# A decoder layer with routed experts: rows gathered expert by expert, down projection split along its contraction, mixing on 32-row groups

## The reference, cut to what matters

```
p = rms_norm(x) @ w_in                       # 2048 -> 6144 columns
x = x + [attention | gated short conv] @ w_out
h = rms_norm(x)
g_star = argmax(h @ w_rg + b_rg)             # 1 of 4 groups
w, e_idx = top 2 of 8 experts in the group   # softmax weights
y = sum over the two experts of
      w * (silu(h @ w_gate[e]) * (h @ w_up[e])) @ w_down[e]
x = x + y
```

## Time and profile before

| | us |
|---|---|
| median of 3 runs (1517.11 to 1518.77) | 1518.23 |
| the profiled execution | 1517.3 |
| its span | 1515.5 |
| PE busy (88% of the span) | 1340.8 |
| DVE busy (26%) | 388.9 |
| ACT busy (14%) | 212.9 |
| POOL busy (4%) | 60.4 |

### The profile page before, as it was taken

How to read it: one execution, slowest core, us unless ns; L and a number is a source line. 1 busy time by engine, 2 the same in 40 slices (tenths; PEclk the granted TensorE clock), 3 DMA queues, 4 the chain that set the end, 5 groups by cost and what they waited for, 6 DMA issues and landing times.

```text
span 1515.5 us, 19525 instructions
## 1 busy us (share of the span) xinstructions
PE 1340.8 (88%) x8104; PEld 907.2 (60%) x8104; DVE 388.9 (26%) x842; ACT 212.9 (14%) x555; POOL 60.4 (4%) x65
## 2 busy tenths in 40 slices
PE   6999999999899968888978979869869879878887
PEld 6888888888677756446437437436426526535542
DVE  3333137765111141121122113103103113113112
ACT  4111231321001121100110110100100110110110
POOL 0000003312010000000000000000000000000000
PEclk9999999999999979889899879889889979979988
DMA  9965334637694326999999999999999999999997
GB/s 296 355 209 181 133 126 157 235 112 261 216 364 176 139 84 248 421 422 419 424 422 423 418 425 422 420 421 424 423 419 423 423 421 419 425 423 420 421 424 294
DMA packets 135644, 503.39 MB, mean 332 GB/s; under 512 B 6214, under 2 KB 80638, under 8 KB 118702
## 3 DMA queue, kind: packets, MB, share of 16 engines
q1 hardware_dynamic: 125670, 495.25, 82.3%
q10 hardware_dynamic: 9600, 6.95, 1.4%
q0 software_dynamic: 336, 0.67, 0.2%
HBM read 496.35 MB, written 6.53 MB: 332 GB/s over the span
## 4 chain that ended last, share of the span: by engine, by line
PE 69%; DMA 19%; SPq 5%; DVE 4%; issue 2%; ACT 1%; POOL 0%; ACTq 0%; DVEq 0%; POOLq 0%
PE bank L600 28%; PE bank L807 11%; PE bank L794 10%; DMA ring<-in_w_down 10%; DMA ring<-in_w_up 7%; PE bank L866 7%; PE bank L845 5%; PE bank L830 4%; SPq L482 4%; DMA ring<-in_cache_v 1%; DVE bc L1411 1%; DVE cat L1406 1%; DMA xa<-in_x_prompt 1%; PE bank L750 1%; PE bank L834 1%
## 5 line engine op out<-in xcount | busy, mean ns | idle before, releaser
L600 PE MATMUL bank<-bc,ring 128*128 128x264 f32 x1536 | 350.8, 387 | 0.0
L794 PE MATMUL bank<-ring,cat 128*32 128x512 f32 x2048 | 266.0, 652 | 77.5 <-DMA ring<-in_w_gate 36.0
L600 PEld LDWEIGHTS bank<-bc,ring 128*128 128x128 f32 x1536 | 288.2, 190 | 50.0 <-issue 0.8
L866 PE MATMUL bank<-ring,bc 128*32 128x256 f32 x2048 | 180.1, 523 | 37.9 <-DVE bc L1413 28.7
L794 PEld LDWEIGHTS bank<-ring,cat 128*32 128x32 f32 x2048 | 61.9, 115 | 217.4 <-issue 120.7
L807 PEld LDWEIGHTS bank<-bc 128*128 128x128 f32 x768 | 169.4, 311 | 15.8 <-issue 14.9
L845 PEld LDWEIGHTS bank<-consts,bc 128*128 128x128 f32 x512 | 124.3, 327 | 88.7 <-DVE bc L1411 56.9
L807 PE MATMUL bank<-bc 128*128 128x128 f32 x768 | 170.4, 383 | 5.6 <-DVE bc L1375 5.6
L866 PEld LDWEIGHTS bank<-ring,bc 128*32 128x32 f32 x2048 | 87.0, 147 | 118.8 <-issue 82.4
L845 PE MATMUL bank<-consts,bc 128*128 128x32 f32 x512 | 131.5, 401 | 26.1 <-DVE bc L1411 26.1
L600 PE MATMUL bank<-cat,ring 128*128 128x264 f32 x512 | 117.9, 389 | 0.0
(11 more groups left out here) (234 smaller groups left out, 596.1 us busy)
## 6 DMA issues: line engine op xcount, KB each, us to landing
ring<-in_w_gate SPq DMA_DIRECT2D x64, 2048.0 KB, 23.4
ring<-in_w_up SPq DMA_DIRECT2D x64, 2048.0 KB, 23.2
ring<-in_w_down SPq DMA_DIRECT2D x64, 2048.0 KB, 27.8
ring<-in_w_in SPq DMA_DIRECT2D x24, 2048.0 KB, 13.3
ring<-in_w_out SPq DMA_DIRECT2D x8, 2048.0 KB, 17.9
ring<-in_cache_k SPq DMA_DIRECT2D x16, 512.0 KB, 4.8
ring<-in_cache_v SPq DMA_DIRECT2D x16, 512.0 KB, 12.4
ring<-qrows_scratch SPq DMA_DIRECT2D x2, 2048.0 KB, 7.4
```

The costliest lines, as they stand in the source:

```text
L600: m = pe.matmul(bank[n % 3][:, 0:T], w[:, k, (i % TPU) * P:(i % TPU + 1) * P], src[:, k, :], start=n_k == 0, stop=n_k == KT - 1)
L794: m = pe.matmul(bank[b][c * C:(c + 1) * C, :], xeT[:, 8 * i + k, j * C:(j + 1) * C], w[:, k, :], start=i == 0 and k < 4, stop=i == 1 and k ...
L866: m = pe.matmul(bank[2 + 2 * i][n * C:(n + 1) * C, 0:256], actT[:, c, :], w[:, c, n, :], start=c == 0, stop=c == FC - 1, skip_group_check= ...
```

## The change

- **Start.** The first weight unit is issued right after x, in two halves, without waiting for the small vectors. The constants come in two parts (the second on SP after the first unit), and the small vectors and the sample rows are loaded by ACT. x is turned in groups of four tiles of 128 columns per bank, and the sums of squares are split between ACT and DVE.
- **`w_out` tiles.** The residual sum stays turned (`yT` over `hT`, read back from DRAM in the turned form), the three transposes a tile, the row squares and POOL's copies go. Router products come in pairs on two column groups. After the last tile, twelve `y_turn`s of four transposes and one ACT copy each build `h2`.
- **Router.** Logits are used unscaled by the norm; fewer steps lead to the slot numbers; `select` is done for the first expert's 32 slots first.
- **Expert loop.** Each expert is gathered by itself (12 matmuls of 32 x 128 by 512 columns), while the expert before is worked on; ACT copies the rows, PE turns them (`turn_rows`), DVE scales them (`gain`). A down unit holds two of the four contraction chunks for all columns, so that its rows in DRAM are one run. `ye` of one expert lies on four groups of 32 rows, one for each 512 columns, and is mixed for that expert alone, with contractions of 32 rows, between the next expert's units.
- **End.** Five `mix` steps of the last expert, each 512 columns stored by itself.

```diff
@@ SP, start
-            sp.wait_ge(vecs_in, VECS * 16)
-            sp.wait_ge(consts_in, 16)
             for n, (kind, u) in enumerate(FRONT):
                 s = slot_of(n)
+                if n == 0:
+                    w0 = w_in[:, :, COLUMN[kind]:COLUMN[kind] + UC]
+                    to = ring[:, s, :].rearrange("p (k c) -> p k c", k=KT)
+                    sp.dma_start(to[:, 0:KT // 2, :], w0[:, 0:KT // 2, :]).then_inc(w0_half, 16)
+                    sp.dma_start(to[:, KT // 2:, :], w0[:, KT // 2:, :]).then_inc(slot_full[s], 16)
+                    sp.dma_start(consts[:, NFIRST:], ins["consts"][:, NFIRST:]).then_inc(consts2_in, 16)
+                    continue
@@ SP, the units of an expert
-            wd = ins["w_down"].rearrange("l (g j) (p k) d -> (l g) p j k d", j=EG, k=FC)
+            wd = ins["w_down"].rearrange("l (g j) (p k) d -> (l g) p j (k d)", j=EG, k=FC)
...
-                    src = wd[bass.ds(g, 1), :, j, :, half * (D // 2):(half + 1) * (D // 2)].rearrange("o p k d -> p (o k) d")
+                src = (wg, wu, wd)[i // 2][bass.ds(g, 1), :, j, half * UNIT:(half + 1) * UNIT].rearrange("o p n -> p (o n)")
@@ PE, W tiles
             for j in range(KT):
                 tile(TILE_AT[("W", j)])
-                if j >= 1:
-                    y_turn(j - 1)
-            y_turn(KT - 1)
+                if j >= 2 and j % 2 == 0:
+                    router_products(j - 2)
+                    router_products(j - 1)
+            router_products(KT - 2)
+            y_turn(Y_ORDER[0], (0, 1))
+            router_products(KT - 1)
+            y_turn(Y_ORDER[0], (2, 3))
@@ PE, new functions
+            def gather(j, it):
...
+                for t in range(TT):
+                    if it is None:
+                        pe.wait_ge(sel_ready, t + 1)
+                    for c in range(4):
+                        cols = slice(c * 512, (c + 1) * 512)
+                        if t < 2:
+                            lhs, rhs = sel[:, t, j * C:(j + 1) * C], h2[:, t, cols]
+                        else:
+                            lhs, rhs = sel[0:NB, t, j * C:(j + 1) * C], h2s[:, cols]
+                        m = pe.matmul(bank[4][c * C:(c + 1) * C, :], lhs, rhs, start=t == 0, stop=t == TT - 1, skip_group_check=True)
+                m.then_inc(gathered, 1)
+            def turn_rows(e):
+                pe.wait_ge(xrow_copied, e)
+                for m_ in range(4):
+                    m = pe.transpose(bank[5][:, m_ * P:(m_ + 1) * P], xrow[:, m_ * P:(m_ + 1) * P], ident)
+                m.then_inc(xe_T, 1)
...
+                    def down(j, i):
+                        w = weights(j, 4 + i).rearrange("p (c d) -> p c d", c=FC // 2)
+                        for c in range(FC // 2):
                             for n in range(4):
+                                m = pe.matmul(bank[2][n * C:(n + 1) * C, :], actT[:, i * FC // 2 + c, :], w[:, c, n * 512:(n + 1) * 512],
+                                              start=i == 0 and c == 0, stop=i == 1 and c == FC // 2 - 1, skip_group_check=True)
+                        m.then_inc((down_half, down_done)[i], 1)
+                    def mix(step):
+                        t, h, j = step
+                        to = MIX_BANKS[step]
+                        for n in range(4) if t == 2 else (2 * h, 2 * h + 1):
+                            rows_ = slice(n * C, (n + 1) * C)
+                            if t == 2:
+                                m = pe.matmul(bank[to[0]][rows_, :], gateT[rows_, 2, 0:C], ye[rows_, :],
                                               start=True, stop=True, skip_group_check=True)
+                            else:
+                                m = pe.matmul(bank[to[n % 2]][:, :], gateT[rows_, t, :], ye[rows_, :], start=True, stop=True)
                         m.then_inc(mixed, 1)
@@ PE, an expert
+                        unit_products(j, 0, 0)
                         if j >= 1:
+                            pe.wait_ge(ye_copied, e)
+                            if j >= 2:
+                                adds_done((2, None, j - 2))
+                            mix((0, 0, j - 1))
+                        unit_products(j, 0, 1)
+                        if j >= 1:
+                            adds_done((0, 0, j - 1))
+                            mix((0, 1, j - 1))
                         unit_products(j, 1, 0)
...
+                        fold(0, g_sb, g_copied, e)
+                        if j >= 1:
+                            adds_done((0, 1, j - 1))
+                            mix((1, 0, j - 1))
+                        gather((j + 1) % EG, it)
+                        if j >= 1:
+                            adds_done((1, 0, j - 1))
+                            mix((1, 1, j - 1))
                         unit_products(j, 1, 1)
...
+                            adds_done((1, 1, j - 1))
+                        for t in range(TT):
+                            for c in range(4):
+                                m = pe.matmul(bank[5][c * C:(c + 1) * C, t * P:(t + 1) * P], gate[:, t, j * C:(j + 1) * C], ident,
+                                              start=True, stop=True, skip_group_check=True)
+                        m.then_inc(gate_T, 1)
+                        if j >= 1:
+                            mix((2, None, j - 1))
+                        fold(1, u_sb, u_copied, e).then_inc(folded, 1)
+                        pe.wait_ge(gateT_copied, e + 1)
+                        turn_rows(e + 2)
                         pe.wait_ge(act_ready, e + 1)
+                        down(j, 0)
+                        down(j, 1)
```

804 lines of the change are left out of this document (448 added, 356 removed).

## The result

| | median us | runs | profiled execution | span | clock |
|---|---|---|---|---|---|
| before | 1517.67 | 4 | 1517.30 | 1515.5 | 0.923 |
| after | 1473.40 (1472.21 to 1476.16) | 4 | 1472.74 | 1470.9 | 0.936 |

The ratio is 0.9711 [0.9695, 0.9728]: 44.3 us faster. The forecast was 1463, its range 1451 to 1486. The sign and most of the mechanism were right; the size was 10 us too good.

The account below looks back on a forecast made before the run. The prediction took PE as the bound ahead of the expert loop and weight transfers at 422 GB/s within it. Terms -7.5 - 11 - 12 - 9 - 15 - 1 = -55.5 gave 1461.8, plus 0.9 for the median 1463; range 1451 to 1486.

Parts of the forecast that it names:

- start: Kernel begin: first weight unit issued right behind x, first tile read by ACT at 22.5 for 30.0 us, -7.5.
- `w_out` tiles: The 16 `w_out` tiles: without turns and with paired router products they take 118.6 for 129.4 us, -11.
- router, first gather: From the last `w_out` tile to the first expert unit read: 19 us where 31 were, -12.
- hole and layout: Expert weight stream: -9 from no pause behind the first unit, -15 from down units in 16 KB runs at 429 GB/s.
- PE's loop: Expert loop on PE: 102 us a group, hidden under 117.3 us of transfers, 15 us left, cost 0.
- tail: Kernel end, from last weight read to last addition's end: 8.3 for 9.0 us, -1.
- rival A: Expert weight stream keeps its 422 GB/s despite 16 KB runs: 1478 us, chance 0.15.
- Rival C: Expert loop: mixes on 32 rows don't overlap at all, +24 us a group, 1536 us, chance 0.05.
- first half of B: Expert loop: the sample tile's four mixes into one bank run singly, +2.6 an expert; whole rival 1485 us, chance 0.14.
- The other half of B: Expert loop: PE and its clock dips set the pace, 119 to 121 us a group; whole rival 1485 us, chance 0.14.
- The lower end of the range: Whole kernel: 1451 us, from bounds of start, tiles and router said to give some 12 below the forecast.

Follow-up runs that it names:

- e_tail2: Changed kernel with the next expert's gather ahead of the first up unit and the gate turn with the sample's mix ahead of the second: 1512.39 us against 1473.40.
- e_order: Changed kernel with the matmul for the ranks behind all eight turns of the prompt's rows in place of the sixth: 1471.78 us against 1473.40.
- e_pad: Changed kernel with 48 one-column matmuls that nothing reads, and a wait for VectorE's last additions before them, at each group's head: 1489.99 us against 1473.40.
- e_hole: Changed kernel with four extra gathers between the first and second unit product of every group: 1498.22 us against 1473.40.
- e_gfirst: Changed kernel with the gather for the next expert moved ahead of the first up product, nothing added: 1473.32 us against 1473.40.
- e_best: Changed kernel with the gather ahead of the first up product and the ranks' matmul behind two more turns: 1473.94 us against 1473.40.
- e_gatewait: Changed kernel with the wait for the experts' gate moved between the first expert's first and second weight units, nothing added: 1480.27 us against 1473.40.

## Why the prediction was right, and where it was not

The span fell by 44.6; from one profile each, by the forecast's own terms:

| term | forecast | measured | how |
|---|---|---|---|
| start | -7.5 | -5.8 | first tile starts 21.92, 16.13; read by ACT 30.06, 25.07 (-5.0) |
| between, not forecast | 0 | -2.2 | 391.6, 389.4 from first tile to first `w_out` tile |
| `w_out` tiles | -11 | -9.9 | 129.4, 119.5 (405.56 to 525.09) |
| router, first gather | -12 | -9.3 | last tile to first unit read: 31.1, 21.8 |
| hole and layout | -24 | -22.4 | first unit read to last landing: 926.7, 904.3 |
| PE's loop | 0 | 0 | waits for weights stay |
| tail | -1 | +5.0 | last landing to the end: 14.7, 19.7 |

The line "between" is chance: the twelve profiles with the changed kernel's code up to there have 389.4 to 395.1, and the changed kernel's own is the shortest. Of the terms, the layout and the hole are shown by runs that change them alone; start, tiles and router are read from the two traces.

- **The stream** (-24) was right in sum and in its parts: undoing the layout alone cost 16.4 for the 15 forecast (13.7 by the landings), and a gap of 12.3 us between the first two loads cost 6.9 for 7.4 by the rule that gave the 8.9. By the Trainium skill, "DMA: Bandwidth & Descriptors", opening table, transfers from 512 B on have line rate, which the prediction made rival A. That doesn't hold here for the last few per cent: with down units in pieces of 4 KB a group moves 422 GB/s, with 16 KB 428.
- **Rival C and the first half of B** fell. A pair of mixes (L919 x4) takes 1.13 us and a set of four on one bank (L916 x8) 1.06 (874.69 in the changed kernel): 32-row contractions overlap, and the set into one bank does too. The other half of B, a loop paced by PE, is what e_tail2 became; the changed kernel still waits for weights in every group but the first. By the rule of the Trainium skill, "TensorEngine Tiling (Array Packing)", Restrictions and Gotchas, that different row tiles can't access one PSUM bank at the same time, the set would have been serial; here four row tiles write four different groups of 32 partitions of one bank, and no run shows what they do on the same partitions.
- **PE's loop** had a cost of 0 and has it, but by less than the "15 us left" said. PE is busy 106.7 a group, where 102 were forecast, and waits 5 to 9 for weights; the bound that I compared with (117.3) is the stream's pace without the ring's lead, and with it the estimate is 114.5.
- **The failed step is the tail**, -1 forecast and +5.0 measured, over half of the 10 us missed. "From the last weight read to the last addition's end" was forecast to 8.3 and is 7.4 (1459.3 to 1466.7). What I took as given is that PE reads the last weights as they land. Already before, it read them 2.3 us after (landing 1500.75, read 1503.04): the prediction says that the second half of the last down product "had waited", but its 64 records follow each other without a gap. Now it is 8.1. The work between the landing of the last expert's first up unit (1436.5) and the last down unit read (unit, fold, mix, gather, mix, unit, gate turn, mix, fold, turn, product, two units) takes 22.7 us, while only three more units of 4.89 land.
- **Two things make that chain long, and the clock is the larger.** In e_order, e_pad and e_hole the same chain takes 18.8 us, at a granted clock of 1.00; in the changed kernel's profile the clock is 0.77, and 3.9 us of the 22.7 are that (before, the clock was 0.80 there). At full clock the chain is still 4.1 longer than the three landings: work that fills PE's waits inside the loop can't be hidden behind the last units. Of the 5.8 us that the lag grew, 1.9 are therefore put down to the longer chain and 3.9 to the clock, which differs from one execution to the next (the same code has lags of 4.6 to 9.1 in the table). My expectation for e_gfirst blamed the work alone. It doesn't settle it: its lag was 5.3, but with a chain at a clock of 0.91, and e_best, with the same move, has 9.8; both have a new wait for VectorE of 1.39 in the last expert. So the split is read from traces, and no experiment shows that less work there shortens the time.
- **Router and first gather**: the first gather began 13.1 us after the last tile (525.09 to 538.23), as forecast, though released by the last of the twelve copies that I had put under the small steps, since PE waited for the ranks with six turns queued behind. What was short is the part behind it, 8.7 us for 6: 5.3 for 4 up to the first unit, and that unit at half the clock, 3.4 for 1.9. e_order takes 1.5 us out of the whole stretch in its profile; its median doesn't show it.
- **Start**: the first tile starts at 16.13 for the 14.4 that -7.5 would give, and ACT reads it at 25.07 for 22.5. The root waited for DVE's sum of squares of the sample rows, 2.3 us in a place where I had counted half a sum. ACT's read stood behind its exponential, which waited 4.12 us for DVE and so for the last of the vector loads, a delay that the prediction had put at nothing. This is read from the trace alone.
- **The lower end of the range** rests on a sum that doesn't come out: the bounds of start, tiles and router give 2.5 + 2 + 4 = 8.5 below the forecast, and the 12 only with those of layout (2) and tail (1).

## What to carry to other kernels

Where the stream of weights sets the pace, look for its shape first (runs of 16 KB in place of 4 KB for a third of the weights: 16.4 us of 1490) and for anything between the reads of the first two slots: of such a pause all but one unit's transfer is paid. Work that is put into an engine's idle places inside a loop can come out again behind the last iteration: follow the last iteration by itself, from the landing of its first late input, and at both levels of the clock. And measure how far an engine is from being the bound by adding work to it, with a look at the loop's head: past a certain length of the body each turn of the loop has a price of its own.

## What the runs showed of the hardware

- DMA packets of 4096 bytes took 163.6 ns, those of 16384 bytes 615; a unit of 2 MiB in the first kind landed 5.12 us after the one before it, in the second 4.89.
- A loop body with 1,504 matmul and weight load records turned without a gap, bodies with 1,696 and 1,888 stood 5.3 to 5.9 us at each turn, one with 1,600 at three of seven.
- Four matmuls with contractions of 32 rows, on four row groups, into four partition groups of one bank: 1.06 us, no more than a pair into two banks (1.13).
- Waits of PE of 1.0 to 1.4 us were followed by work at half the clock (1.2 for 2.4 GHz) in some places: 1.90 us for a pair of 1.13 in e_tail2, 3.31 for a unit of 1.92 in e_gatewait. Not everywhere: the changed kernel's unit at 898.2 us had waited 1.4 and ran at full clock.
- One chain of PE's work at the end of the loop took 18.8 us at a granted clock of 1.00 and 22.7 at 0.77.
- Matmuls of one column took 35 to 41 ns a record in e_pad (3.36 us for 95 records, 3.08 for 75), one after the other, with a weight load for each. That is no cheap filler: 16 records of 512 columns, four side by side, take 1.92.
